# Attention over the paged cache moved into the prompt's loop over heads, in four column groups of 32

## What is computed

```python
h = rms_norm(x); u, q, k, v, qi, ki, wi = split(h @ w_in)
conv = silu(layer_norm(depthwise_conv(u, width=31)))         # 512 channels
sel  = top_k(sum_h wi * relu(qi . ki), 256)                  # keys that a query may see
attn_prompt = softmax(q k^T / 8 over sel) v                  # 1024 queries x 1024 keys, causal
attn_sample = softmax(q [k_past, k_new]^T / 8 over sel) [v_past, v_new]
x = x + concat(conv, attn) @ w_out                           # 1088 rows x 1024
x = x + (silu(n(x) @ w_gate) * (n(x) @ w_up)) @ w_down       # width 2816
```

## Time and profile before

| | us |
|---|---|
| median of three runs (range) | 1784.83 (1778.36 to 1784.87) |
| the profiled execution | 1782.72 |
| its span, first to last instruction | 1780.9 |
| TensorE busy | 1592.3 (89%) |
| VectorE / ScalarE / POOL busy | 900.8 / 443.2 / 468.2 |
| mean granted TensorE clock, share of full | 0.939 |
| attention loop, about | 505 to 762 |
| sample attention stage | 762 to 873.4 |
| output product | 873.4 to 975 |
| feed-forward | 975 to 1780.9 |

### The profile page before, as it was taken

The page is one execution under the profiler, slowest core; times in us unless marked ns, Lnnn a source line. Parts: engine busy times, 40 slices in busy tenths (PEclk is TensorE's granted clock), DMA queues, the critical chain, the costliest instruction groups (busy, mean ns, idle before and its releaser), DMA issues.

```text
span 1780.9 us, 24226 instructions
## 1 busy us (share of the span) xinstructions
PE 1592.3 (89%) x8977; PEld 1445.7 (81%) x8977; DVE 900.8 (51%) x1620; ACT 443.2 (25%) x807; POOL 468.2 (26%) x322
## 2 busy tenths in 40 slices
PE   3999988879957879855798999999999999999999
PEld 3998767437846768722598999999999999999999
DVE  5299889998668874420124343341332423424323
ACT  4100268654256435421113101001010010010100
POOL 4332211311320000022023324324334343252320
PEclk9999999889968768867899999999999999999999
DMA  6212101210230010046511011111111111111102
GB/s 201 78 37 74 52 12 28 60 33 24 70 129 19 6 51 1 1 139 187 178 48 48 25 48 48 40 31 59 36 46 47 35 47 47 35 47 47 47 0 100
DMA packets 120728, 100.75 MB, mean 57 GB/s; under 512 B 12137, under 2 KB 107689, under 8 KB 120519
## 3 DMA queue, kind: packets, MB, share of 16 engines
q1 hardware_dynamic: 112346, 91.74, 16.8%
q10 hardware_dynamic: 8309, 8.08, 1.4%
HBM read 87.13 MB, written 13.02 MB: 56 GB/s over the span
## 4 chain that ended last, share of the span: by engine, by line
PE 51%; DVE 2%; issue 2%; SPq 1%; ACT 1%; DMA 0%; ACTq 0%; DVEq 0%
PE ps L818 16%; PE ps L820 16%; PE ps L819 16%; PE ps L1210 1%; PE ps L1168 1%; DVE f_lo L2233 1%; SPq L504 0%; DVE lo_t L2177 0%; DVE x L2240 0%; SPq L628 0%; DMA kt_b<-in_cache_kt 0%; DVE lo_t L2100 0%; PE ps L1194 0%; DVE mx L2142 0%; SPq L512 0%
## 5 line engine op out<-in xcount | busy, mean ns | idle before, releaser
L818 PE MATMUL ps<-hi_t,w_hi 128*128 128x384 f32 (+3 forms) x1464 | 480.0, 328 | 10.6 <-DVE lo_t L2177 4.8
L820 PE MATMUL ps<-hi_t,w_lo 128*128 128x384 f32 (+3 forms) x1464 | 479.4, 327 | 0.0
L819 PE MATMUL ps<-lo_t,w_hi 128*128 128x384 f32 (+3 forms) x1464 | 479.2, 327 | 0.0
L818 PEld LDWEIGHTS ps<-hi_t,w_hi 128*128 128x128 f32 (+1 forms) x1464 | 275.4, 188 | 12.1 <-issue 6.4
L819 PEld LDWEIGHTS ps<-lo_t,w_hi 128*128 128x128 f32 (+1 forms) x1464 | 275.4, 188 | 0.6
L820 PEld LDWEIGHTS ps<-hi_t,w_lo 128*128 128x128 f32 (+1 forms) x1464 | 275.2, 188 | 0.6
L2240 DVE TENSOR_TENSOR x<-x,ps 128x384 f32<-128x384 f32 (+1 forms) x264 | 139.3, 530 | 107.4 <-PE ps L820 106.5
L818 PE MATMUL ps<-f_hi,w_hi 128*128 128x384 f32 (+1 forms) x528 | 176.0, 333 | 2.4 <-DVE x L2240 2.2
L819 PE MATMUL ps<-f_lo,w_hi 128*128 128x384 f32 (+1 forms) x528 | 173.5, 329 | 0.0
L820 PE MATMUL ps<-f_hi,w_lo 128*128 128x384 f32 (+1 forms) x528 | 173.5, 329 | 0.0
L801 POOL CAST w_hi<-w_raw 128x1024 fp32r<-128x1024 f32 x60 | 62.5, 1041 | 339.3 <-PE ps L820 339.3
(11 more groups left out here) (284 smaller groups left out, 2418.2 us busy)
## 6 DMA issues: line engine op xcount, KB each, us to landing
w_raw<-in_w_in SPq DMA_DIRECT2D x24, 512.0 KB, 3.7
w_raw<-in_w_gate SPq DMA_DIRECT2D x22, 512.0 KB, 3.7
w_raw<-in_w_up SPq DMA_DIRECT2D x22, 512.0 KB, 3.7
w_raw<-in_w_down SPq DMA_DIRECT2D x22, 512.0 KB, 3.5
kt_b<-in_cache_kt SPq DMA_DIRECT2D x64, 128.0 KB, 2.4
v_b<-in_cache_v SPq DMA_DIRECT2D x40, 128.0 KB, 3.6
x<-in_x_t SPq DMA_DIRECT2D x8, 544.0 KB, 6.8
xin<-in_x_prompt SPq DMA_DIRECT2D x8, 512.0 KB, 4.3
```

What stands on the lines that cost most here:

```text
L818: pe.matmul(out, a_hi, b_hi, start=first, stop=False)
L819: pe.matmul(out, a_hi, b_lo, start=False, stop=False)
L820: return pe.matmul(out, a_lo, b_hi, start=False, stop=last)
```

## The change

`SAMPLE_AT = (8, 24, 40, 56)`: the four pairs are worked inside the loop over heads. At n = 8, 24, 40, 56 TensorE makes a pair's scores ahead of that iteration's own; one iteration later it turns the weights, seven later it multiplies with the values, nine later it turns the outputs. A pair is four column groups of 32: two sequences times two halves of the key/value heads, each with 4 heads x 8 tokens. A matmul of the values is then 128 columns wide rather than 256, and there are twice as many. The scores of all 8 sequences' new keys are one product with 64 columns, masked by `smx`.

The prompt's scores at n = 8 and 24 go to bank 3 meanwhile; at n = 40 and 56 they need two banks, and come only when the exponential of the pair is taken. The buffer of the prompt's scores shrinks from four to three. Keys and values of a sequence share one buffer (for one of the two it is the raw weight buffer), so the values are loaded when the scores are made and the next keys when the values are used; the last pair has buffers of its own where the taps' inputs were. The first two key loads stand in front of the reload of the taps' inputs in SP's queue. The sample queries are turned at n = 2, their block-diagonal form `q_blk` made at n = 4.

The third norm block leaves the loop: its three steps, and the last tile's output transposes, stand between the first output products, which start with blocks 0 and 1. The step of VectorE for the norm stands at the head of its iteration, not at its end.

```diff
+OUT_ORDER = [(0, 0), (0, 1), (1, 0), (1, 1), (2, 0), (2, 1), (0, 2), (1, 2), (2, 2)]
+OUT_ORDER += [(m, j) for m in range(3, KT) for j in range(NB)]
-LN_AT = (46, 48, 50, 55, 57, 58, 63, 65, 66)
+LN_AT = (46, 49, 50, 54, 56, 58)
+SAMPLE_AT = (8, 24, 40, 56)
+SROWS = NKV // 2 * TS * 2
@@ SP
+            sp.wait_ge(split_lo, N_OUT)
+            load_keys(0, 0, pages_now[0])
             sp.wait_ge(proj_done, BASE[5])
             load_queries(0)
             load_queries(1)
+            sp.wait_ge(kt_ps, 1)
+            sp.wait_ge(stores, 16 * 4)
+            load_keys(0, 1, pages_now[1])
...
             sp.dma_start(u_a[0][:, :], u_scr[:, 0, :]).then_inc(u_back, 16)
@@ TensorE
+            def sample_scores(pr):
+                n = SAMPLE_AT[pr]
...
+                pe.wait_ge(sm_done, n - 1)
+                for j, (a, z) in enumerate([(0, 512), (512, PAST), (PAST, PAST + SR)]):
+                    if j == 2:
+                        pe.wait_ge(sm_done, n)
+                    for par, part, rows in groups(pr):
+                        keys = sample_buffers(pr)[0][par][:, part, a:z] if j < 2 else k_t[:, part, :]
+                        pe.matmul(ps[rows, j, 0:z - a], q_blk[:, 2 * pr + par, part, :], keys, start=True, stop=False)
+                    mm = pe.matmul(ps[:, j, 0:z - a], kb[0:SR, P + 2 * pr * SR:P + (2 * pr + 2) * SR],
+                                   smneg[:, a:z] if j < 2 else smx[:, :], start=False, stop=True)
+            def sample_values(pr):
...
+                pe.wait_ge(qt_lo, min(S // P, n // NH + 2))
...
+                for c in range(NPG + 1):
+                    for par, part, rows in groups(pr):
+                        cols = slice(part * P, (part + 1) * P)
...
+                        mm = pe.matmul(ps[rows, 7, 384:512], w, v, start=(c == 0), stop=(c == NPG))
             for n in range(NA + 4):
-                if n < NA:
+                if n in SAMPLE_AT:
+                    sample_scores(SAMPLE_AT.index(n))
+                late = n in SAMPLE_AT and n // NH >= 4
+                if n < NA and not late:
                     scores(n)
+                if n - 1 in SAMPLE_AT:
+                    sample_turn(SAMPLE_AT.index(n - 1))
+                    values(n - 3)
                 if n >= 2 and n - 2 < NA:
                     turn(n - 2)
...
+                if late:
+                    scores(n)
+                if n - 7 in SAMPLE_AT:
+                    sample_values(SAMPLE_AT.index(n - 7))
@@ output product on TensorE
+                if s == 0:
+                    output_transposes(S // P - 1)
+                if 1 <= s <= 3:
+                    layer_norm_sum(5 + s)
@@ VectorE, in the loop
+                if n - 1 in LN_AT:
+                    layer_norm_step(LN_AT.index(n - 1))
+                if n in SAMPLE_AT:
+                    sample_max(SAMPLE_AT.index(n))
                 if n < NA:
                     mask_scores(n)
```

More of the change, by code:

```diff
@@ L90 @@
 EARLY, LATE = 3, 2
+SAMPLE_AT = (8, 24, 40, 56)
+SROWS = NKV // 2 * TS * 2
+QUERY_ORDER = [0, SAMPLE] + list(range(1, S // P))
 def rows_of(t):
@@ L505, in page_numbers, with score_place, sample_buffers @@
                     for j in range(NPG)]
[L507 to L514, removed]
+        def score_place(n, keys):
+            first = 3 if n in SAMPLE_AT and keys <= 512 else 2 * (n % 2)
+            return wide(first, keys)
+        def sample_buffers(pr):
+            return (late_k, late_v) if pr == NS // 2 - 1 else (kt_b, v_b)
         block = ctx.enter_context(nc.Block())
@@ L594, in _, with load_queries @@
                                  ).then_inc(kis_in[b], 16)
-            for n in range(19, 27):
+            for n in range(19, 25):
                 load_unit(n)
-            def load_queries(i):
+            def load_queries(place):
+                i = QUERY_ORDER[place]
                 r = rows_of(i)
@@ L632, in _ @@
[L632 to L655, removed]
+            load_queries(2)
@@ new lines, in _ @@
+            load_queries(3)
+            load_queries(4)
+            for pr in range(NS // 2):
+                if pr > 0:
+                    pages_now = page_numbers(sp, 2 * pr), page_numbers(sp, 2 * pr + 1)
+                    if pr == NS // 2 - 1:
+                        sp.wait_ge(tap_done, CT * W)
+                        sp.wait_ge(stap_done, 3 * CT)
+                    for par in range(2):
+                        load_keys(pr, par, pages_now[par])
+                    if pr == NS // 2 - 1:
+                        sp.wait_ge(spv_done, pr)
+                        load_unit(N_OUT)
+                        load_unit(N_OUT + 1)
+                    else:
+                        load_queries(2 * pr + 4)
+                for par in range(2):
+                    load_values(pr, par, pages_now[par])
+                if pr < 2:
+                    load_queries(2 * pr + 5)
@@ L656, in _ @@
+            load_unit(N_OUT + 2)
+            load_unit(N_OUT + 3)
+            sp.wait_ge(pv_done, NH * (S // P))
+            sp.wait_ge(sm_done, NH * (S // P))
+            sp.wait_ge(spv_done, NS // 2)
             for m in range(KT):
                 sp.dma_start(x1[:, m, :], A["x_t"][m * P:(m + 1) * P, :]).then_inc(x_in[m // 4], 16)
+            for n in range(N_OUT + 4, N_FFN):
+                load_unit(n)
             gv = A["w_gate"].rearrange("(k p) f -> p k f", p=P)
@@ L1102, in layer_norm_sum @@
                 a, z = BLOCKS[k]
+                n = LN_AT[v] if v < len(LN_AT) else NA + 4
+                pe.wait_ge(spt_ready, 2 * sum(at + 1 <= n for at in SAMPLE_AT))
+                pe.wait_ge(so_ready, sum(at + 7 <= n for at in SAMPLE_AT))
+                pe.wait_ge(sot_ready, sum(at + 9 <= n for at in SAMPLE_AT))
                 if v == 0:
@@ L1132, in layer_norm_sum, with groups @@
                         r = rows_of(t)
-                        mm = pe.matmul(ps[:, 7, t * P - a:t * P - a + r], ones[0:r, :], lnd[0:r, t % 3, 0:r],
+                        mm = pe.matmul(ps[:, 7, t * P - a:t * P - a + r], ones[0:r, :], (lnd, lnd_2)[k // 2][0:r, t % 3, 0:r],
                                        start=True, stop=True)
                     mm.then_inc(lnb_mm, 1)
+            def groups(pr):
+                for par in range(2):
+                    for part in range(2):
+                        g = 2 * par + part
+                        yield par, part, slice(g * SROWS, (g + 1) * SROWS)
@@ L1146, in _ @@
+                if n - 9 in SAMPLE_AT:
+                    sample_outputs(SAMPLE_AT.index(n - 9))
+                if n == 2:
+                    query_transposes(SAMPLE)
+                if n % NH == 5 and n < NA - NH:
                     query_transposes(n // NH + 1)
```

444 lines of the change are left out of this document (235 added, 209 removed).

## The result

The changed kernel takes 1709.1 us (median of 4 runs, 1708.6 to 1712.1) where the kernel before took 1784.9 in the same comparison: a ratio of 0.9587, with a 95% interval of 0.9569 to 0.9605. The profiled execution took 1708.57 us with a span of 1706.5, against 1782.72 and 1780.9. The forecast was 1716, the range 1690 to 1746.

A forecast was written before the change was run, and what follows sets the result against it. VectorE's taps, then TensorE, bound the loop; sample attention was a chain of waits; TensorE bound the output product. Removing 115.0 us and adding 47.5 (55.5 less 8 absorbed) took 1782.7 to 1715.2, given as 1716, range 1690 to 1746.

The forecast's parts named there:

- The solid part: Last head's turned weights to last product before norm: 218.4 us become 105.8; with a mean product leaving the loop, 115.0 less.
- The 5.0 to the first product: From `values(63)` to the first output product: values, VectorE's outputs, block 0's parts and hand-overs, 5.0 us (3.5 to 8).
- R4: Output product: the norm does not hide behind the products, 6 us more; chance 0.60 together with the forecast.
- Late taps: Start of the convolution's taps: their inputs queue behind the second sequence's keys on SP, adding 4.4 us (0 to 7).
- Values: Sample value products in the loop: 5.5 us a pair in 72 records, none hidden on TensorE, 20.8 us added in all.
- R1: Sample work in the loop: the four column groups run side by side, 21.8 us less, 1694; chance 0.20.
- The bound from below, 3.0: Sample values of a pair: at least 3.0 us, from 0.04 to 0.05 us for each record with hardly any columns.
- Scores: Sample scores in the loop: 4.0 us a pair at full clock level (bounds 2.7 and 5.2), 8.5 us added in all.
- the prompt's scores behind the exponential: At n = 40 and 56 the prompt's scores wait for the pair's maximum and exponential: 4.2 us added.
- R2: Loop: no gain from more groups and TensorE at its half clock level, 30.5 us more, 1746; chance 0.17.
- R3: Page loads set the pace, 12.3 us each; slower than before from five and a half of eight exposed; chance 0.03.

The follow-up runs named there:

- run 8: Changed kernel with the last tile's outputs and third norm block back ahead of the first output product on TensorE: 1726.8 us.
- Run 6: Changed kernel with the second sequence's key loads moved behind the reload of the taps' data on SP's queue: 1707.9 us.
- run 1: Changed kernel with a pair's value products issued group by group instead of chunk by chunk over the four groups: 1740.8 us (one execution).
- run 2: Changed kernel with the value products alternating between only two groups at a time, the other two behind them: 1722.7 us (one execution).
- run 9: Changed kernel without TensorE's sample score products and eight of nine chunks of the sample value products, everything else kept: 1699.1 us.
- run 5: Changed kernel with the second norm block's sums back at the places of the kernel before: 1706.0 us.
- Runs 10 and 11: An exponential added ahead of the changed kernel's feed-forward loop, 1711.5 us; the loop's own function called ahead of it in the kernel before, 1782.8 against 1784.4 us.
- run 7: Changed kernel with the second norm block at its old places and the second sequence's key loads behind the taps' data: 1705.9 us.
- run 3: Changed kernel with sample scores issued group by group over the three banks, their mask wait ahead of all: 1717.1 us (one execution).

## Why the prediction was right, and where it was not

- **The solid part held.** From `values(62)` to the end of the last product before the norm it now takes 895.0 - 788.46 = 106.6 us; 105.8 were forecast. The 5.0 to the first product was meant from `values(63)`, and from there 4.7 are measured (790.31 to 795.02). Since the row taken was `values(62)`, one turn of 1.9 us was missing from the sum: by its own terms the forecast was that much too low. The norm block does hide: no product waits for block 2. R4's price of 6 us for the lost cover was mis-sized; run 8 gives 18.
- **Late taps:** the first tap moved from 513.54 to 517.80, 4.3 against 4.4 forecast. Run 6 shows the whole of it at the first two pairs, and 1.2 us, within the noise, in the time.
- **Values: 5.5 us a pair forecast, 2.4 measured** at the full level, and 11.4 in all against 20.8. This is the term that failed most. It kept the streaming of two groups and added 0.052 us for each record, worked out from 5.08 / 32 = 0.159. That row was a mixture of the two levels of the clock, so the 0.052 was the clock and not a cost of the record; runs 1 and 2 show no such cost. The same misreading made the argument against R1, that two groups "gave only 1.5" at 256 columns. The bound from below, 3.0, fell too: it came from records in two groups, and four share a set. The first pair at the half level took 3.64 + 0.65, close to the forecast for another reason.
- **Scores: 4.0 forecast, about 3.1 for the last pair,** masks included (737.33 to 740.41), within the bounds of 2.7 and 5.2.
- **The clock was a term at nothing.** The forecast left the prompt's products as they were. They took some 12 us less in the changed kernel's loop (208 against 220), at 0.82 instead of 0.79.
- **R1 had the right mechanism, and its number was missed by the waits.** It gave 1694, and its concurrency holds, yet the time is 1709. TensorE waits 18 us more in the loop than before. VectorE's pace does not halve what TensorE saves there: in run 9 the waits stay the same in sum and the clock takes the rest, and in run 1, where the values' records grow by some 28 us, the distance from the first scores to the first output product grows by 27.
- **What filled the gap** were waits that the forecast had priced low or not at all: the norm block's new place (3 us by run 5), the third bank of scores behind the mask (4.5 in three waits), the prompt's scores behind the exponential (6.7 in four, 4.2 forecast). Values priced too dear and a clock that rose stand on one side, these waits on the other. They nearly cancel, which is why `values(62)` came within 5 us of its place; that the sum was right owes much to luck.
- **R2** did not occur: nothing ran one group after the other, though run 1 shows what that costs, 1741, near R2's 1746. **R3** needed five and a half exposed loads and none is; even doubled, one is.
- **Behind the output product** 2.9 us were gained that nobody forecast. Runs 10 and 11 clear the missing table loads, the obvious suspect, and run 7 shows the same code spreading by as much.

Split by part: the interleaving of the last block is worth some 18 us (run 8), and four groups against two in the values 6 to 14 (run 2, one execution). The rest, over 40, is the stage whose waits now lie beside the prompt's work; that part was not tested by itself. The variants that beat the changed kernel do so by 3 us, less than their times can tell: the norm block at its old places (1706.0), alone or with the keys moved (1705.9).

## What to carry to other kernels

Narrow products in separate column groups are worth interleaving chunk by chunk, so that neighbours belong to different groups: the same instructions in another order cost 32 us here. When work moves into a loop, compare the records of the work that was already there: here they changed by 8 to 12 us with the clock, in either direction, and a run that took 17 us or more of TensorE's records away gained only 10 though TensorE's waits did not grow in sum. Before a row becomes a price, look at the clock that was granted in it. And before a vanished instruction is credited with a gain, put it back: the eleven table loads cost nothing.

## What the runs showed of the hardware

- Column groups of 32 ran four at a time with nothing lost at 128 moving columns: 16, 32 and 64 records in 1.93 to 1.95 us. At 512 columns a set of records side by side took some 0.44 us whether it held two or four (1.94 us for four sets of two, 1.06 for two sets of four).
- The mean granted clock of the loop was 0.79 in the kernel before, 0.82 in the changed one, 0.78 without the sample products (run 9) and 0.84 with longer score records (run 3); the same prompt products took 220, 208, 218 and 200 us of records. No run shows what sets it.
- The granted clock in the loop differs between executions of nearly the same code. At the second pair's values it was at the full or at the half level (1.95 or 3.64 us for the same 64 records), and that alone took back a lead of some microseconds. A place reached earlier in a trace is no gain until the next stretch with a steady clock has been read too.
